# Expert output of 896 streamed and 1152 gathered columns, with second-half differences made by GpSimd

## The chip, the cores and the metric

The kernel runs on one core of a Trainium2 chip. The metric is the device time of one execution in microseconds (us), as a median over runs; lower is better. TensorE, VectorE, ScalarE and GpSimd are named PE, DVE, ACT and POOL in the profile, and SP is the queue that issues most of the plain DMAs.

## The reference

The reference is a three-layer model on 256 tokens of width 2048: a retention layer, a latent attention layer, and a layer with two kinds of attention followed by a mixture of 16384 small experts. The change touches only the end, the output of the experts. Cut to what matters:

```python
experts = i1 * 128 + i2                       # 128 picks a token: 8 heads x top 16
gates = softmax(top_vals)
u = take(expert_down, experts)                # (token, 128, 2048)
hdn = gelu(einsum('ted,td->te', u, x))
v = take(expert_up, experts)                  # (token, 128, 2048)
y = einsum('te,ted->td', gates * hdn, v)      # added to the residual
out = rms_norm(h + y, final_norm_gain)
```

All is float32. A token's output is the sum of 128 rows of `expert_up`, each scaled by one coefficient.

## The kernel before, in words

The 256 tokens are two halves of 128, `t` = 0 and 1, with one token on each partition. Each engine runs an instruction list of its own in program order; named semaphores (`built`, `rows_used`, ...) order the engines against each other. `sig.at(key)` is what a waiter waits for, `sig.to(key)` is what a producer raises.

**Down rows.** POOL gathers 256 times (`n` = 128 t + pick) one row of `expert_down` for each partition (line 625, `in_peer_down`), and DVE takes the product with the token's input (line 1611). This raises `rows_used` 0 to 255.

**Up rows, in two ways.** The 2048 output columns are split at `DCOL`. The right part, `D - DCOL` columns, is gathered: POOL fetches 256 times one row a partition into one of `NU` buffers (line 637, `in_up_rows`), and DVE adds it, scaled by the coefficient, to the residual `X` (line 1624), which raises `rows_used` 256 to 511. POOL may run `NU` gathers ahead of DVE. The left part, `DCOL` columns, is done as a dense product: all 16384 rows are streamed by SP as 128 blocks of 128 rows (line 573, `in_up_blocks`) through `NS` buffers, and PE multiplies each block by a coefficient matrix (line 2166). The sum over the 128 blocks stays in four PSUM banks.

**Coefficient matrices.** For that product every token's 128 coefficients have to stand at the place of their experts among 16384. An expert is (first half i1, second half i2). For four tokens at a time (a step `q`, 32 steps for each `t`) two 128 x 128 tables a token are made: `OH1`, in which pick e has its coefficient at column i1, and `OH2`, with a one at column i2. PE multiplies the two (line 2149, four products, raises `built`) and ACT copies the result out (line 981, `store`). The tables come from differences: `compare` lets PE write, for each half, pick number minus column number into a PSUM bank (lines 2125 and 2127, a pair for each half). For `t` = 0 ACT turns both differences into tables. For `t` = 1, the stage that the change is about, DVE makes `OH1` from its bank (line 1632, raises `first_hot_v`), and ACT makes `OH2` from its own (lines 999 and 1003, raise `second_hot`). Both have two buffers, so that step q waits for `built` of step q - 2.

**Order in the build stage of t = 1.** DVE's list interleaves the two jobs:

```python
if 2 <= n < 34:
    q = n - 2
    ...
    v.wait_ge(*built.at(fours[30 + q]))
```

`fours[30 + q]` is step q - 2 of `t` = 1. One scaled addition stands before each table. POOL's list holds only gathers in this stretch. When step 31 is built, PE spreads the final gain (line 2157) and then runs through the 128 blocks. At the end DVE adds the four banks to `X` (line 1640), ACT sums squares (lines 1015, 1022), and DVE scales and SP writes out.

Of the kernel before, what the change touches and what calls it, by code (L numbers as in the profile page):

```python
# [14 lines left out]
D = 2048  # L15
NG = 8
DCOL = 1024
NU = 6
NS = 4
EPS = 1e-6  # L20
# [92 lines left out]
def flat(x):  # L113
    return x.rearrange("p a b -> p (a b)")


def build(nc, A, out):
    ctx = ExitStack()
    with ctx:
# [137 lines left out]
        EF = [GBA[:, 512 + 256 * t:768 + 256 * t].rearrange("p (i j) -> p i j", i=2) for t in range(2)]  # L257
        EFR = [at(kept_end + 256 * t, 2, 128, of=arena_r) for t in range(2)]
        STEP, LESS, IDR, ONER = (at(kept_end + 512 + 128 * i, 128, of=arena_r if i else arena) for i in range(4))
        assert kept_end + 1024 <= LBO + 4 * 384, kept_end  # L260
        gbuf = [at(RAWS + i * 2048, D) for i in range(NG)]

        ubuf = [at(144 * KB + 1024 * i, D - DCOL) for i in range(2)] + [at(YG + 1024 * i, D - DCOL) for i in range(4)]
        sbuf = [at(W + 4096 + DCOL * i, DCOL) for i in range(NS)]
        OH1 = [at(152 * KB + 512 * i, 4, 128) for i in range(2)]
# [154 lines left out]
        d_g = [dma_sig(f"d_g{i}", range(32)) for i in range(NG)]  # L420
        d_u = [dma_sig(f"d_u{i}", range(43)) for i in range(NU)]
        d_s = [dma_sig(f"d_s{i}", range(32)) for i in range(NS)]

# [88 lines left out]
        first_hot_a, first_hot_v = sig("first_hot_a", fours[0:32]), sig("first_hot_v", fours[32:])  # L512
        compared, less_read, second_hot = sig("compared", fours), sig("less_read", fours), sig("second_hot", fours)
        built, stored = sig("built", fours), sig("stored", fours)
        block_used = sig("block_used", range(127))
# [30 lines left out]
        def sync(sp):  # L546
# [9 lines left out]
            for i, (kind, n, fn, info) in enumerate(plan):  # L556
# [10 lines left out]
                for dst, src in fn(raws[i % 8]):  # L567
                    sp.dma_start(dst, src).then_inc(wsem[i % 8], 16)
            sp.wait_ge(*gate_made.at(1))
            for b in range(128):  # L570
                if b >= NS:
                    sp.wait_ge(*block_used.at(b - NS))
                sp.dma_start(sbuf[b % NS], up_blocks[b]).then_inc(*d_s[b % NS].to(b // NS))
# [6 lines left out]
        def gpsimd(g):  # L580
# [38 lines left out]
            for n in range(256):  # L619
                i, t, j = n % NG, n // 128, n % 128  # L620
                if j % 64 == 0:
                    g.wait_ge(*chosen.at((t, j // 64)))
                if n >= NG:
                    g.wait_ge(*rows_used.at(n - NG))
                g.indirect_dma_start(  # L625
                    out=gbuf[i], out_offset=None, in_=down,
                    in_offset=bass.IndirectOffsetOnAxis(ap=EI[t][:, j:j + 1].bitcast(U32), axis=0)
                ).then_inc(*d_g[i].to(n // NG))
            for n in range(256):
                i, t, j = n % NU, n // 128, n % 128  # L630
                if n == 0:
                    g.wait_ge(*picks_rounded.at(1))
                elif n == 2:
                    g.wait_ge(*rows_used.at(255))
                if n >= NU:
                    g.wait_ge(*rows_used.at(256 + n - NU))
                g.indirect_dma_start(  # L637
                    out=ubuf[i], out_offset=None, in_=up_rows,
                    in_offset=bass.IndirectOffsetOnAxis(ap=EI[t][:, j:j + 1].bitcast(U32), axis=0)
                ).then_inc(*d_u[i].to(n // NU))  # L640


        def scalar(s):
# [329 lines left out]
            for t in range(2):  # L973
                s.wait_ge(*chosen.at((t, 1)))
                s.copy(flat(EFR[t]), flat(EF[t])).then_inc(*picks_rounded.to(t))  # L975

# [6 lines left out]

            for t in range(2):
                s.wait_ge(*rows_used.at(128 * t + 127))
                s.activation(HD[t], HD[t], ACT.Gelu_apprx_tanh).then_inc(*gelud.to(t))
# [4 lines left out]
                for q in range(33):  # L991
                    o1, o2 = OH1[q % 2], flat(OH2[q % 2])
                    if q < 32:
                        s.wait_ge(*compared.at((t, q)))
                        if 32 * t + q >= 2:
                            s.wait_ge(*built.at(fours[32 * t + q - 2]))
                        if t == 0:
                            s.activation(flat(o1), bank[q % 2], ACT.Abs)
                        s.activation(o2, bank[2 + q % 2], ACT.Abs).then_inc(*less_read.to((t, q)))
# [18 lines left out]
            for t in range(2):  # L1018
                for b in range(2):
                    c = 24 + 3 * t + 1 + b  # L1020
                    s.wait_ge(*dense_added.at(2 * t + b))
                    r = s.activation(GBB[:, 0:512], X[:, t, b * 512:(b + 1) * 512], ACT.Square, scale=float(D) ** -0.5,
                                     accum_out=st[:, c:c + 1])
# [7 lines left out]
        def vector(v):  # L1031
# [587 lines left out]
            for n in range(256):  # L1619
                t, j = n // 128, n % 128  # L1620
                v.wait_ge(*d_u[n % NU].at(n // NU))
                if n:
                    v.wait_ge(*rows_used.at(256 + n - 1))
                v.scalar_tensor_tensor(out=X[:, t, DCOL:], in0=ubuf[n % NU], scalar=HD[t][:, j:j + 1], in1=X[:, t, DCOL:],  # L1624
                                       op0=ALU.mult, op1=ALU.add).then_inc(*rows_used.to(256 + n))
                if 2 <= n < 34:
                    q = n - 2
                    if q == 0:
# [7 lines left out]
            for t in range(2):  # L1636
                for b in range(2):
                    xs = X[:, t, b * 512:(b + 1) * 512]
                    v.wait_ge(*dense_made.at(2 * t + b))
                    v.tensor_tensor(xs, bank[2 * t + b], xs, ALU.add).then_inc(*dense_added.to(2 * t + b))  # L1640
            v.wait_ge(*gain_made.at(0))
# [15 lines left out]
        def tensor(pe):  # L1657
# [460 lines left out]
            def compare(t, q):  # L2118

                if q == 0:  # L2120
                    pe.wait_ge(*picks_rounded.at(t))
                for p in range(2):
                    b = 2 * p + q % 2
# [5 lines left out]
                free[q % 2] = first_hot_v.at((1, q)) if t else less_read.at((0, q))  # L2129
                free[2 + q % 2] = less_read.at((t, q))  # L2130

            pe.wait_ge(*rounded.at(0))
            take(6)
            take(7)
            for t in range(2):
                compare(t, 0)
                take(4 + t)
# [24 lines left out]
            for i2 in range(128):  # L2162
                pe.wait_ge(*d_s[i2 % NS].at(i2 // NS))
                for t in range(2):
                    for b in range(2):
                        r = pe.matmul(bank[2 * t + b], coef_of(t, i2), sbuf[i2 % NS][:, b * 512:(b + 1) * 512],  # L2166
                                      start=i2 == 0, stop=i2 == 127)
# [38 lines left out]
```

## Time and profile before

| what | value |
|---|---|
| device time, median of 3 runs | 3396.77 us (3392.41 to 3396.88) |
| the profiled execution, its own time | 3395.3 us |
| its span, first to last instruction | 3393.5 us |
| gather of down rows ends (last of line 1611) | 2784.2 us |
| build stage of t = 1 | 2785 to 2932.6 us |
| stream of the up blocks on PE | 2938.6 to 3380.3 us |
| TensorE clock, mean over the span | 0.826 |

Times in the table are from the start of the span. The profile has rows for each instruction and, for a stretch, the busy time of every engine, the clock that TensorE was granted (1.00 is 2.4 GHz), the busy share of the 16 DMA engines and the bytes that they moved. An idle time in square brackets stands ahead of the instruction, with what ended it.

### The profile page before, as it was taken

Reading aid. Unit: us, or ns where it says so; the run is one execution under the profiler, and the core shown is the slowest. Engines: PE = TensorE matmul, PEld = TensorE weight load, DVE = VectorE, ACT = ScalarE, POOL = GpSimd, SP = SyncE. Lnnn points to the kernel's source line nnn. Section 1 sums busy time; section 2 is a strip of 40 time slices with the busy share of each in tenths; the row PEclk is TensorE's granted clock in tenths of the full one; section 3 lists DMA queues with packets and bytes.
Section 4 is the critical chain, followed back from the end, with each engine's and each line's share of the span. In section 5 each row is a group of like instructions: output and inputs, shape, how many; then the busy total and the mean of one; then the engine's idle time right before and its main releaser. Section 6 shows DMA issues by size and latency. Waiting matters only on the chain.

```text
span 3393.5 us, 34746 instructions
## 1 busy us (share of the span) xinstructions
PE 2632.1 (78%) x13316; PEld 2068.8 (61%) x13316; DVE 2259.6 (67%) x3026; ACT 1013.4 (30%) x1649; POOL 827.0 (24%) x581
## 2 busy tenths in 40 slices
PE   3789999989989989799997984000098019999998
PEld 3689999977869877798875884000055006544443
DVE  6877777776754455444434458999999984566666
ACT  2233433443444444443334441000087004200000
POOL 5500000000000000000000003733588871345443
PEclk9789999999999999798985987555555555699999
DMA  8768777767856435364330544999999994699998
GB/s 295 258 216 265 266 260 260 250 230 246 286 150 171 134 101 165 100 184 128 114 113 25 174 149 184 377 360 352 345 421 421 422 385 122 217 409 409 409 409 336
DMA packets 340693, 858.35 MB, mean 253 GB/s; under 512 B 38072, under 2 KB 97728, under 8 KB 306864
## 3 DMA queue, kind: packets, MB, share of 16 engines
q1 hardware_dynamic: 265872, 447.54, 39.8%
q0 software_dynamic: 74656, 408.60, 30.9%
q8 instruction: 105, 1.72, 0.2%
q14 instruction: 60, 0.49, 0.0%
HBM read 853.95 MB, written 2.10 MB: 252 GB/s over the span
## 4 chain that ended last, share of the span: by engine, by line
PE 52%; DVE 12%; POOL 8%; issue 3%; ACT 2%; DMA 1%; DVEq 0%; ACTq 0%; POOLq 0%
PE ps L2166 13%; PE ps L1666 10%; PE ps L1668 9%; PE ps L1667 9%; POOL s L625 8%; DVE s L1611 7%; PE ps L2149 2%; PE ps L2127 1%; PE ps L2046 1%; PE ps L2125 1%; PE ps L1927 1%; DMA s<-in_peer_down,s 1%; PE ps L2048 1%; DVE s L1521 0%; DVE s L1512 0%
## 5 line engine op out<-in xcount | busy, mean ns | idle before, releaser
L1666 PE MATMUL ps<-r,r 128*128 128x256 f32 (+2 forms) x3248 | 1065.5, 328 | 81.3 <-DVE r L1044 42.3
L1044 DVE TENSOR_TENSOR r<-s,r 128x1024 fp32r<-128x1024 f32 (+1 forms) x532 | 647.2, 1221 | 616.1 <-ACT r L652 615.6
L1667 PE MATMUL ps<-r,r 128*128 128x256 f32 (+2 forms) x3248 | 1047.2, 322 | 0.0
L1668 PE MATMUL ps<-r,r 128*128 128x256 f32 (+2 forms) x3248 | 1046.3, 322 | 0.0
L652 ACT CAST r<-s 128x1024 fp32r<-128x1024 f32 (+1 forms) x532 | 551.3, 1039 | 954.4 <-PE ps L1668 910.2
L1666 PEld LDWEIGHTS ps<-r,r 128*128 128x128 f32 x3248 | 642.7, 198 | 137.5 <-DVE r L1044 40.3
L1667 PEld LDWEIGHTS ps<-r,r 128*128 128x128 f32 x3248 | 643.1, 198 | 43.6 <-issue 4.6
L1668 PEld LDWEIGHTS ps<-r,r 128*128 128x128 f32 x3248 | 642.0, 198 | 41.0
L1611 DVE CUSTOM_DVE_ANT_0 s<-s,s 128x2048 f32<-128x2048 f32 x256 | 583.8, 2285 | 30.9 <-DMA s<-in_peer_down,s 30.7
L625 POOL DMA_INDIRECT s<-in_peer_down,s x256 | 473.1, 1848 | 448.6 <-DVE s L1569 238.0
L1624 DVE SCALAR_TENSOR_TENSOR s<-s,s,s 128x1024 f32<-128x1024 f32 x256 | 328.6, 1284 | 163.9 <-DMA s<-in_up_rows,s 162.4
L2166 PE MATMUL ps<-s,s 128*128 128x512 f32 x896 | 392.1, 595 | 0.0
L2125 PE MATMUL ps<-r 128*128 128x512 f32 x128 | 100.5, 785 | 353.7 <-ACT r L975 353.7
L637 POOL DMA_INDIRECT s<-in_up_rows,s x256 | 251.9, 984 | 346.6 <-DVE s L1624 323.1
L2166 PEld LDWEIGHTS ps<-s,s 128*128 128x128 f32 x896 | 170.9, 191 | 215.3 <-issue 215.3
L2125 PEld LDWEIGHTS ps<-r 128*128 128x128 f32 x128 | 39.8, 311 | 381.9 <-ACT r L972 353.9
L610 POOL DMA_DIRECT2D s<-in_final_norm_g x1 | 0.6, 625 | 1093.5 <-DVE s L1393 1093.5
L1062 DVE SCALAR_TENSOR_TENSOR s<-s,s,s 128x512 f32<-128x512 f32 x304 | 226.7, 783 | 2.5 <-DMA s<-in_ada_w 1.1
L2139 PE MATMUL ps<-s 128*128 128x128 f32 x2 | 0.9, 448 | 200.0 <-DVE s L1616 200.0
L2149 PE MATMUL ps<-s 128*128 128x128 f32 x512 | 132.4, 441 | 5.8 <-ACT s L1008 3.1
L2149 PEld LDWEIGHTS ps<-s 128*128 128x128 f32 x512 | 113.9, 327 | 33.3 <-issue 20.6
L1015 ACT ACTIVATE s<-s 128x1024 f32<-128x1024 f32 x2 | 2.1, 1056 | 442.3 <-DVE s L1624 442.3
(259 smaller groups left out, 2123.3 us busy)
## 6 DMA issues: line engine op xcount, KB each, us to landing
s<-in_ada_w SPq DMA_DIRECT2D x192, 512.0 KB, 5.4
s<-in_ret_w_in SPq DMA_DIRECT2D x128, 512.0 KB, 5.4
s<-in_up_blocks SPq DMA_DIRECT2D x128, 512.0 KB
s<-in_w_in SPq DMA_DIRECT2D x96, 512.0 KB, 3.7
s<-in_ret_w_in SPq DMA_DIRECT2D x128, 256.0 KB, 3.9
s<-in_ret_w_out SPq DMA_DIRECT2D x64, 512.0 KB, 5.1
s<-in_mla_w_in SPq DMA_DIRECT2D x48, 512.0 KB, 3.7
s<-in_mla_w_out SPq DMA_DIRECT2D x32, 512.0 KB, 3.7
```

What stands on the lines that cost most here:

```text
L625: g.indirect_dma_start(out=gbuf[i], out_offset=None, in_=down, in_offset=bass.IndirectOffsetOnAxis(ap=EI[t][:, j:j + 1].bitcast(U32), axis ...
L637: g.indirect_dma_start(out=ubuf[i], out_offset=None, in_=up_rows, in_offset=bass.IndirectOffsetOnAxis(ap=EI[t][:, j:j + 1].bitcast(U32), a ...
L652: s.copy(hi_of(w), raw_of(w)).then_inc(*hi_made.to(w))
L1044: v.tensor_tensor(lo_of(w), raw_of(w), hi_of(w).bitcast(F), ALU.subtract).then_inc(*lo_made.to(w))
L1062: r = v.scalar_tensor_tensor(out=acc[h], in0=w, scalar=cact[:, k:k + 1], in1=acc[h], op0=ALU.mult, op1=ALU.add)
L1611: v.tensor_tensor_reduce(gbuf[n % NG], gbuf[n % NG], HN[:, t, :], 1.0, 0.0, ALU.mult, ALU.add, HD[t][:, j:j + 1]).then_inc(*rows_used.to(n))
L1624: v.scalar_tensor_tensor(out=X[:, t, DCOL:], in0=ubuf[n % NU], scalar=HD[t][:, j:j + 1], in1=X[:, t, DCOL:], op0=ALU.mult, op1=ALU.add).th ...
L1666: pe.matmul(o, lh, rh, start=start, stop=False, skip_group_check=True)
L1667: pe.matmul(o, lh, rl, start=False, stop=False, skip_group_check=True)
L1668: return pe.matmul(o, ll, rh, start=False, stop=stop, skip_group_check=True)
L2149: r = pe.matmul(bank[b][:, k * 128:(k + 1) * 128], OH1[q % 2][:, k, :], OH2[q % 2][:, k, :], start=True, stop=True)
L2166: r = pe.matmul(bank[2 * t + b], coef_of(t, i2), sbuf[i2 % NS][:, b * 512:(b + 1) * 512], start=i2 == 0, stop=i2 == 127)
```

## The change

`DCOL` goes from 1024 to 896. So a block of the stream has 896 columns (448 for each of the four products of a block), and a gathered row has 1152. The gathered rows have 5 buffers in place of 6, the stream 3 in place of 4, and both lie elsewhere. In the build stage of `t` = 1 DVE does two scaled additions for each table. The second difference there is no longer written by PE: PE turns the second halves of the picks once, ACT copies them to `SECOND`, and POOL subtracts them from the column numbers (`less`), straight into `OH2`, where ACT works in place. `less` stands in POOL's list behind every second gather. The diff, cut to its core:

```diff
-DCOL = 1024
-NU = 6
-NS = 4
+DCOL = 896
+HCOL = DCOL // 2
+NU = 5
+NS = 3
...
         def sync(sp):
             sp.wait_ge(*gate_made.at(1))
+            sp.wait_ge(*picks_rounded.at(1))
+            sp.wait_ge(*second_copied.at(0))
             for b in range(128):
...
         def gpsimd(g):
+            def less(q):
+
+                g.wait_ge(*built.at(fours[30 + q]))
+                g.tensor_tensor(OH2[q % 2], STEP.unsqueeze(1).broadcast_to([128, 4, 128]),
+                                SECOND[:, 4 * q:4 * q + 4].unsqueeze(2).broadcast_to([128, 4, 128]),
+                                ALU.subtract).then_inc(*second_less.to((1, q)))
+
+            g.wait_ge(*gate_made.at(1))
             for n in range(256):
                 i, t, j = n % NU, n // 128, n % 128
-                if n == 0:
-                    g.wait_ge(*picks_rounded.at(1))
-                elif n == 2:
+                if n == 2:
+                    g.wait_ge(*second_copied.at(0))
+                    g.wait_ge(*d_step.at("all"))
+                    less(0)
+                    less(1)
                     g.wait_ge(*rows_used.at(255))
                 if n >= NU:
                     g.wait_ge(*rows_used.at(256 + n - NU))
...
                 ).then_inc(*d_u[i].to(n // NU))
+                if n % 2 == 0 and 2 <= n // 2 < 32:
+                    less(n // 2)
...
         def scalar(s):
                     if q < 32:
-                        s.wait_ge(*compared.at((t, q)))
-                        if 32 * t + q >= 2:
-                            s.wait_ge(*built.at(fours[32 * t + q - 2]))
-                        if t == 0:
+                        if t:
+                            s.wait_ge(*second_less.at((1, q)))
+                            s.activation(o2, o2, ACT.Abs).then_inc(*less_read.to((t, q)))
+                        else:
...
         def vector(v):
                 v.scalar_tensor_tensor(out=X[:, t, DCOL:], in0=ubuf[n % NU], scalar=HD[t][:, j:j + 1], in1=X[:, t, DCOL:],
                                        op0=ALU.mult, op1=ALU.add).then_inc(*rows_used.to(256 + n))
-                if 2 <= n < 34:
-                    q = n - 2
+                if n % 2 and n // 2 - 1 in range(32):
+                    q = n // 2 - 1
                     if q == 0:
                         v.wait_ge(*coef_copied.at(1))
                     v.wait_ge(*built.at(fours[30 + q]))
...
         def tensor(pe):
-                for p in range(2):
+                for p in range(2 - t):
                     b = 2 * p + q % 2
...
+                if t:
+                    take(5)
+                    pe.transpose(bank[5][:, 0:128], EF[1][:, 1, :], IDN).then_inc(*second_turned.to(0))
+                    free[5] = second_copied.at(0)
                 compare(t, 0)
```

The rows below are instruction lists, without times; names in brackets are the semaphores that a row waits for. POOL, at the end of the down gathers and the start of the up gathers, before (`in_up_rows` is the gathered part, `s144_57` and `s112_55` hold its buffers):

```order
L637 DMA s144_57<-in_up_rows,s192_60 128x1024 [waits picks_rounded]
L637 DMA s144_57<-in_up_rows,s192_60 128x1024
L637 DMA s112_55<-in_up_rows,s192_60 128x1024 [waits rows_used]
L637 DMA s112_55<-in_up_rows,s192_60 128x1024 x3
L637 DMA s144_57<-in_up_rows,s192_60 128x1024 [waits rows_used] x2
L637 DMA s112_55<-in_up_rows,s192_60 128x1024 [waits rows_used] x4
```

The same place on POOL in the changed kernel, where line 653 is the gather and line 638 is `less`:

```order
L653 DMA s160_58<-in_up_rows,s192_60 128x1152 [waits gate_made]
L653 DMA s160_58<-in_up_rows,s192_60 128x1152
L638 TENSOR_TENSOR s144_57<-s192_60 128x512 [waits built,d_step,second_copied]
L638 TENSOR_TENSOR s144_57<-s192_60 128x512 [waits built]
L653 DMA s112_55<-in_up_rows,s192_60 128x1152 [waits rows_used]
L653 DMA s112_55<-in_up_rows,s192_60 128x1152 x2
L638 TENSOR_TENSOR s144_57<-s192_60 128x512 [waits built]
L653 DMA s160_58<-in_up_rows,s192_60 128x1152 [waits rows_used] x2
L638 TENSOR_TENSOR s144_57<-s192_60 128x512 [waits built]
L653 DMA s112_55<-in_up_rows,s192_60 128x1152 [waits rows_used] x2
```

Gathers 0 and 1 stand ahead of `less` 0 and 1, then come gathers 2, 3 and 4, `less` 2, gathers 5 and 6, `less` 3, and so on up to `less` 31 behind gather 62: every second gather now stands behind an instruction that waits for `built`.

DVE, at the start of the build stage of `t` = 1, before (line 1624 is the scaled addition, line 1632 the table `OH1`; `d_u0` and the like are the gathers' landings):

```order
L1624 SCALAR_TENSOR_TENSOR s0_49<-s144_57,s192_60,s0_49 128x1024 [waits d_u0,coef_made]
L1624 SCALAR_TENSOR_TENSOR s0_49<-s144_57,s192_60,s0_49 128x1024 [waits rows_used,d_u1]
L1624 SCALAR_TENSOR_TENSOR s0_49<-s112_55,s192_60,s0_49 128x1024 [waits rows_used,d_u2]
L1632 SCALAR_TENSOR_TENSOR s144_57<-ps,s192_60 128x512 [waits compared,built,coef_copied]
L1624 SCALAR_TENSOR_TENSOR s0_49<-s112_55,s192_60,s0_49 128x1024 [waits rows_used,d_u3]
L1632 SCALAR_TENSOR_TENSOR s144_57<-ps,s192_60 128x512 [waits compared,built]
L1624 SCALAR_TENSOR_TENSOR s0_49<-s112_55,s192_60,s0_49 128x1024 [waits rows_used,d_u4]
L1632 SCALAR_TENSOR_TENSOR s144_57<-ps,s192_60 128x512 [waits compared,built]
```

The same place on DVE in the changed kernel (line 1648 the addition, line 1656 the table):

```order
L1648 SCALAR_TENSOR_TENSOR s0_49<-s160_58,s192_60,s0_49 128x1152 [waits d_u0,coef_made]
L1648 SCALAR_TENSOR_TENSOR s0_49<-s160_58,s192_60,s0_49 128x1152 [waits rows_used,d_u1]
L1648 SCALAR_TENSOR_TENSOR s0_49<-s112_55,s192_60,s0_49 128x1152 [waits rows_used,d_u2]
L1648 SCALAR_TENSOR_TENSOR s0_49<-s112_55,s192_60,s0_49 128x1152 [waits rows_used,d_u3]
L1656 SCALAR_TENSOR_TENSOR s144_57<-ps,s192_60 128x512 [waits compared,built,coef_copied]
L1648 SCALAR_TENSOR_TENSOR s0_49<-s112_55,s192_60,s0_49 128x1152 [waits rows_used,d_u4]
L1648 SCALAR_TENSOR_TENSOR s0_49<-s160_58,s192_60,s0_49 128x1152 [waits rows_used,d_u0]
L1656 SCALAR_TENSOR_TENSOR s144_57<-ps,s192_60 128x512 [waits compared,built]
L1648 SCALAR_TENSOR_TENSOR s0_49<-s160_58,s192_60,s0_49 128x1152 [waits rows_used,d_u1]
```

Table 0 stood behind addition 2 and now stands behind addition 3, table 1 behind addition 5 in place of 3; in general table q stands behind addition 2q + 3 in place of q + 2.

## Rows read from the trace of the kernel before

**Rows 1.** The chain that ended last, from 2922 us on: start us, us, what

```profile
2924.29 2.01 PE ps L2149 x8
2926.30 0.43 PE ps L2125
2926.72 0.72 PE ps L2127
2927.44 0.73 PE ps L2125
2928.17 0.72 PE ps L2127
2928.89 3.69 PE ps L2149 x16
...
2933.51 5.06 PE ps L2157 x32
2938.57 441.72 PE ps L2166 x1024
...
3380.31 0.70 DVE s L1640
```

**Rows 2.** Busy time, clock, DMA share and GB/s, by stretches

```profile
2784.00:2938.50 154.50, 149.75 (x414) 94.98 (x414) 71.62 (x76) 60.43 (x130) 43.01 (x43) 0.51 0.44 138
2938.50:3380.00 441.50, 441.50 (x1025) 195.26 (x1024) 278.87 (x219) 3.65 (x8) 204.52 (x212) 1.00 1.01 401
...
2938.50:2942.00 3.50, 3.50 (x5) 1.50 (x5) 3.29 (x3) 0.00 (x0) 2.59 (x4) 0.50 0.95 341
...
3000.00:3300.00 300.00, 300.00 (x701) 132.82 (x700) 188.48 (x148) 1.15 (x2) 142.56 (x147) 1.00 1.03 409
3300.00:3380.00 80.00, 80.00 (x188) 35.20 (x186) 50.05 (x41) 2.50 (x6) 30.01 (x33) 1.00 0.94 374
```

The columns are the stretch and its length, then PE, PE's weight loads, DVE, ACT and POOL, each with its instructions, then clock, DMA share and GB/s.

**Rows 3.** Groups of instructions in the build stage, 2784 to 2938.5 us

```profile
L637 POOL DMA_INDIRECT s<-in_up_rows,s x43 | 43.2, 1004 | 122.8 <-DVE s L1624 107.2 <-DVE s L1611 11.9 <-issue 3.7
L1632 DVE SCALAR_TENSOR_TENSOR s<-ps,s 128x512 f32<-128x512 f32 x32 | 22.1, 691 | 79.7 <-PE ps L2127 79.7
```

**Rows 4.** Groups of instructions in the stream, 2938.5 to 3380 us

```profile
L1624 DVE SCALAR_TENSOR_TENSOR s<-s,s,s 128x1024 f32<-128x1024 f32 x216 | 277.5, 1285 | 161.2 <-DMA s<-in_up_rows,s 160.4
```

**Rows 5.** Timeline at the start of the build stage, PE, DVE and POOL

```profile
2784.59 0.93 POOL L637 DMA_INDIRECT s<-in_up_rows,s  x1 [11.88 <-DVE s L1611]
2785.03 2.68 DVE L1624 SCALAR_TENSOR_TENSOR s<-s,s,s 128x1024 f32<-128x1024 f32 x2
...
2785.83 1.29 POOL L637 DMA_INDIRECT s<-in_up_rows,s  x1 [0.30 <-issue]
...
2788.86 1.28 DVE L1624 SCALAR_TENSOR_TENSOR s<-s,s,s 128x1024 f32<-128x1024 f32 x1 [1.15 <-DMA s<-in_up_rows,s]
2790.06 0.69 DVE L1632 SCALAR_TENSOR_TENSOR s<-ps,s 128x512 f32<-128x512 f32 x1
...
2790.85 2.04 PE L2149 MATMUL ps<-s 128*128 128x128 f32 x8 [2.67 <-issue]
...
2791.64 1.28 DVE L1624 SCALAR_TENSOR_TENSOR s<-s,s,s 128x1024 f32<-128x1024 f32 x1 [0.89 <-DMA s<-in_up_rows,s]
...
2792.93 0.65 ACT L981 COPY s<-ps 128x256 f32<-128x256 f32 x2 [3.45 <-issue]
```

**Rows 6.** POOL's two-input operation in the first layer, ns min/median/max

```profile
L606 POOL TENSOR_TENSOR s<-s x24: 1260/1340/2905, 23.6 to 175.8; 128x512 f32<-128x512 f32 x24
```

**Rows 7.** Timeline at the first gather of down rows

```profile
2083.99 1.03 POOL L625 DMA_INDIRECT s<-in_peer_down,s  x1 [237.98 <-DVE s L1569]
...
2089.83 2.29 DVE L1611 CUSTOM_DVE_ANT_0 s<-s,s 128x2048 f32<-128x2048 f32 x1 [6.73 <-DMA s<-in_peer_down,s]
```

**Rows 8.** Timeline behind the last table: additions whose gathers had landed

```profile
2929.61 12.39 DVE L1624 SCALAR_TENSOR_TENSOR s<-s,s,s 128x1024 f32<-128x1024 f32 x9
```

**Rows 9.** Timeline within the stream: a gather's issue, and its addition six later

```profile
3000.49 0.94 POOL L637 DMA_INDIRECT s<-in_up_rows,s  x1 [1.60 <-DVE s L1624]
...
3011.61 1.28 DVE L1624 SCALAR_TENSOR_TENSOR s<-s,s,s 128x1024 f32<-128x1024 f32 x1 [0.80 <-DMA s<-in_up_rows,s]
```

More of the change, by code:

```diff
@@ L257, in build @@
         EF = [GBA[:, 512 + 256 * t:768 + 256 * t].rearrange("p (i j) -> p i j", i=2) for t in range(2)]
-        EFR = [at(kept_end + 256 * t, 2, 128, of=arena_r) for t in range(2)]
+        EFR = [at(kept_end + 256 * t, 2 - t, 128, of=arena_r) for t in range(2)]
+        SECOND = at(kept_end + 384, 128)
         STEP, LESS, IDR, ONER = (at(kept_end + 512 + 128 * i, 128, of=arena_r if i else arena) for i in range(4))
@@ L261, in build @@
         gbuf = [at(RAWS + i * 2048, D) for i in range(NG)]
-        ubuf = [at(144 * KB + 1024 * i, D - DCOL) for i in range(2)] + [at(YG + 1024 * i, D - DCOL) for i in range(4)]
-        sbuf = [at(W + 4096 + DCOL * i, DCOL) for i in range(NS)]
+        ubuf = [at(W + 4096 + (D - DCOL) * i, D - DCOL) for i in range(2)] + [at(YG + (D - DCOL) * i, D - DCOL) for i in range(3)]
+        sbuf = [at(144 * KB + DCOL * i, DCOL) for i in range(2)] + [at(W + 4096 + 2 * (D - DCOL), DCOL)]
         OH1 = [at(152 * KB + 512 * i, 4, 128) for i in range(2)]
@@ L420, in build @@
         d_g = [dma_sig(f"d_g{i}", range(32)) for i in range(NG)]
-        d_u = [dma_sig(f"d_u{i}", range(43)) for i in range(NU)]
-        d_s = [dma_sig(f"d_s{i}", range(32)) for i in range(NS)]
+        d_u = [dma_sig(f"d_u{i}", range(52)) for i in range(NU)]
+        d_s = [dma_sig(f"d_s{i}", range(43)) for i in range(NS)]
         hi_made = sig("hi_made", range(NW))
@@ L513, in build @@
         compared, less_read, second_hot = sig("compared", fours), sig("less_read", fours), sig("second_hot", fours)
+        second_turned, second_copied = sig("second_turned", [0]), sig("second_copied", [0])
+        second_less = sig("second_less", fours[32:])
         built, stored = sig("built", fours), sig("stored", fours)
@@ L974, in scalar @@
                 s.wait_ge(*chosen.at((t, 1)))
-                s.copy(flat(EFR[t]), flat(EF[t])).then_inc(*picks_rounded.to(t))
+                s.copy(flat(EFR[t]), flat(EF[t][:, 0:2 - t, :])).then_inc(*picks_rounded.to(t))
             def store(t, q):
@@ L984, in scalar @@
             for t in range(2):
+                if t:
+                    s.wait_ge(*second_turned.at(0))
+                    s.copy(SECOND, bank[5][:, 0:128]).then_inc(*second_copied.to(0))
                 s.wait_ge(*rows_used.at(128 * t + 127))
@@ L993, in scalar @@
                     if q < 32:
-                        s.wait_ge(*compared.at((t, q)))
-                        if 32 * t + q >= 2:
-                            s.wait_ge(*built.at(fours[32 * t + q - 2]))
-                        if t == 0:
+                        if t:
+                            s.wait_ge(*second_less.at((1, q)))
+                            s.activation(o2, o2, ACT.Abs).then_inc(*less_read.to((t, q)))
+                        else:
+                            s.wait_ge(*compared.at((t, q)))
+                            if q >= 2:
+                                s.wait_ge(*built.at((0, q - 2)))
                             s.activation(flat(o1), bank[q % 2], ACT.Abs)
-                        s.activation(o2, bank[2 + q % 2], ACT.Abs).then_inc(*less_read.to((t, q)))
+                            s.activation(o2, bank[2 + q % 2], ACT.Abs).then_inc(*less_read.to((t, q)))
                         s.wait_ge(*less_read.at((t, q)))
@@ L1021, in scalar @@
                     s.wait_ge(*dense_added.at(2 * t + b))
-                    r = s.activation(GBB[:, 0:512], X[:, t, b * 512:(b + 1) * 512], ACT.Square, scale=float(D) ** -0.5,
+                    r = s.activation(GBB[:, 0:HCOL], X[:, t, b * HCOL:(b + 1) * HCOL], ACT.Square, scale=float(D) ** -0.5,
                                      accum_out=st[:, c:c + 1])
@@ L1637, in vector @@
                 for b in range(2):
-                    xs = X[:, t, b * 512:(b + 1) * 512]
+                    xs = X[:, t, b * HCOL:(b + 1) * HCOL]
                     v.wait_ge(*dense_made.at(2 * t + b))
-                    v.tensor_tensor(xs, bank[2 * t + b], xs, ALU.add).then_inc(*dense_added.to(2 * t + b))
+                    v.tensor_tensor(xs, bank[2 * t + b][:, 0:HCOL], xs, ALU.add).then_inc(*dense_added.to(2 * t + b))
             v.wait_ge(*gain_made.at(0))
@@ L2129, in compare @@
                 free[q % 2] = first_hot_v.at((1, q)) if t else less_read.at((0, q))
-                free[2 + q % 2] = less_read.at((t, q))
+                if t == 0:
+                    free[2 + q % 2] = less_read.at((0, q))
             pe.wait_ge(*rounded.at(0))
@@ L2135, in tensor @@
             for t in range(2):
+                if t:
+                    take(5)
+                    pe.transpose(bank[5][:, 0:128], EF[1][:, 1, :], IDN).then_inc(*second_turned.to(0))
+                    free[5] = second_copied.at(0)
                 compare(t, 0)
@@ L2165, in tensor @@
                     for b in range(2):
-                        r = pe.matmul(bank[2 * t + b], coef_of(t, i2), sbuf[i2 % NS][:, b * 512:(b + 1) * 512],
+                        r = pe.matmul(bank[2 * t + b][:, 0:HCOL], coef_of(t, i2), sbuf[i2 % NS][:, b * HCOL:(b + 1) * HCOL],
                                       start=i2 == 0, stop=i2 == 127)
```

## The prediction

> **What bounds the kernel now.** I read the chain that ended last first, since it names what the end of the program hangs on. From 2924 us to 3380 us it is TensorE alone [rows 1]. The reader sees two stages there. In the build stage of t = 1 one step takes 4.60 us (2924.29 to 2928.89): 2.01 us for the four products, and 2.60 us for two pairs of difference products. Then the stream takes 441.7 us for 1024 matmul instructions, 0.4314 us each. The view by stretches says what stands beside it [rows 2]. In the build stage the DMA engines are busy 0.44 of the time. In the stream TensorE is busy in all of its 441.5 us at clock 1.00, and the DMA engines are full as well: 409 GB/s between 3000 and 3300 us. So the stream is held by TensorE with the transfers just behind it, and VectorE waits there 160 us for gathered rows [rows 4]. The build stage is held by TensorE with idle transfers: VectorE waits for a difference product 79.7 us, and GpSimd 107 us for an addition [rows 3].
>
> **Part 1, the stream.** A matmul instruction covers 448 columns for 512, so TensorE needs 1024 x 0.4314 x 0.875 = 386.5 us. The transfers: a block is 128 x 896 x 4 = 0.459 MB, a gather 128 x 1152 x 4 = 0.590 MB (0.524 MB each before). Both numbers matter, since TensorE alone would give back 55 us and the transfers won't.
>
> **Part 2, the build step on each engine.** TensorE loses one pair, 1.45 us of 4.60 [rows 1], and comes to 3.15. VectorE: an addition of 1024 columns takes 1.285 us [rows 4] and 12.39 / 9 = 1.377 us in a row with its overhead [rows 8]; 128 columns more at 1.28 / 1024 us each make it 1.51. Two and a table of 0.69 [rows 3] are 3.7 us. GpSimd: `less` is two-input work on 128 x 512 floats; the trace has the same shape in an addition at 1.34 us, 1.26 to 2.91 [rows 6]. With two gathers at 0.94 and 0.30 between instructions [rows 5, 9] that is 3.8 to 4.1 us. By busy time, then, a step would come to about 4.1 us and the stage would be no longer than now.
>
> **Part 3, the order, which decides.** Table q stands behind addition 2q + 3, and that needs gather 2q + 3. On GpSimd this gather stands behind `less(q + 1)`, which waits for `built` of step q - 1. And `built` of step q waits for table q. So from one `built` to the next everything is in series: `less`, gather issue, landing, addition, table, products. No buffer count loosens it, because GpSimd's list holds the gather back and not a full buffer. Behind the waiting `less(q + 1)` are queued gathers 2q + 3 and 2q + 4, and VectorE waits for them. Before, no gather stood behind `built`. Price of a turn:
> - `built` to the start of `less`: 0.10, an estimate between 0.04 (ACT's copy at 2792.93 behind products that end at 2792.89) and 0.27 us (a gather at 2784.59 behind VectorE) [rows 5].
> - `less`: 1.34, alone on the engines at that moment, since VectorE has finished addition 2q + 2 during the products. Bounds 1.26 and 2.91 [rows 6].
> - gap to the issue: 0.30 [rows 5].
> - issue to the start of its addition: gather 2 was issued at 2784.59 with nothing in flight, and its addition began at 2788.86 after waiting for it: 4.27 us [rows 5]. The wider row adds 0.066 MB at 409 GB/s, 0.16: 4.43. From below: issue of 0.93 and 0.59 MB at 409 GB/s, 2.4 us. From above: the first gather of down rows, 1.05 MB, 5.84 us [rows 7]. I stay with 4.43, the same kind of gather with one just behind it.
> - addition to table: 2788.86 to 2790.06 is 1.20; with 128 more columns 1.33. Table to products 0.79, products 2.04 [rows 5].
>
> The sum is 10.33 us a turn against 4.60.
>
> A landing by the Trainium skill ("DMA: Bandwidth & Descriptors", Anatomy of one DMA, its fit for one gather) would be 2.0 us plus bytes at 436 GB/s, 3.35 us for 0.59 MB, against 4.27 us for the smaller gather in this trace. By it a turn would be 9.25 us and the final time about 32 us under mine; the trace has the duration, so I use that.
>
> **The sum.** Additions 0 and 1 and gathers 2 to 4 start as before. Addition 3 began at 2791.64 [rows 5], now some 0.2 later; table 0 follows at 2793.1, its products end at 2796.0. Thirty turns (gather 63 is the last behind a `less`) are 310 us: `built` of step 30 at 2796 + 310 = 3106. Step 31 needs additions 64 and 65, no `less` between: 3.5 us, 3109.5. The 6.0 us from the last products' end (2928.89 + 3.69) to the stream at 2938.57 stay [rows 1]: stream start 3115.5, 177 us later than before.
>
> Its length: by then some 72 additions are done (66, and six at 1.51 from 3106.6 on) and two more gathers have landed. Left are 182 gathers, 107.3 MB, and 125 blocks, 57.3 MB: 164.7 MB at 409 GB/s are 402.7 us. The whole stream moved 177.0 MB at a mean of 401, where 409 would have needed 432.8; 8.7 us went in its slower start and end (341 and 374 GB/s) [rows 2], and I add them: 411 us. TensorE's 386.5 us lie inside, and the gathers end last. Check by queue: in 386.5 us the blocks take 148 GB/s and leave 261, a gather each 2.26 us, 171 of them; 11 more at VectorE's 1.51 us are 17 us, 403 and the ends. So the stream gives back 441.5 - 411 = 30 us, not 55.
>
> The end: now the last addition follows the last landing (1.4 us), and three bank additions precede the last one (2 us for 448 columns each). Last bank addition 3115.5 + 411 + 3.4 = 3530, and 13.2 us as from 3380.3 to 3393.5: span 3543. Device time stands 1.8 us over the span (3395.3 to 3393.5), so 3545 us; the profiled execution lies 1.5 us under the median, which I leave. The rest costs nothing: the one transpose and ACT's copy of it sit in 168 us in which TensorE is idle (hidden by down gathers; in the open they are below 1 us), `less` 0 and 1 run while GpSimd waits 11.9 us for the last down row [rows 5], and the first blocks load later but 170 us before use.
>
> **Rivals.**
> - *The ring doesn't close* (the change does what busy time allows): I have misread which gather stands behind which `less`, and the step is 4.1 us. For it speaks only Part 2; against it, both lists. 32 steps end at 2790 + 131 + 3, stream from 2930, 30 us shorter, 3.4 later at the end: about 3359 us, faster. The point from which it decides: the stream and the end together give back 30 - 3 = 27 us, so even with the ring the change is no loss if a turn takes no more than (2938.5 + 27 - 2796 - 9.5) / 30 = 5.3 us. Without any gather the ring has 0.10 + 1.34 + 1.33 + 0.79 + 2.04 = 5.6. Chance 4%.
> - *A shorter landing*: issue to addition between 2.4 and 3.7 us. A turn shortens by as much, thirty times: 3.7 gives 3523 us, 2.4 gives 3484. For it speaks that gather 2 had three more behind it in row, where a turn has one; against it, that gather 3, issued 1.24 us later, was not ready before 2791.6 [rows 5]. 13%.
> - *`less` at its slow price*, 2.91 us as when VectorE works beside it: + 1.57 x 30 = 47, 3592 us. Against it, VectorE idles then. 8%.
> - *Three stream buffers are too few*. A gather under full load took 3000.49 to 3011.61, 11.1 us [rows 9]. Were a block as slow (9.5 us with one gather fewer in flight), a block would take (3.0 + 9.5) / 3 = 4.2 us while gathers last: blocks take 0.459 MB / 4.2 us = 109 GB/s, and 182 gathers at 0.590 MB by the other 300 GB/s, 1.97 us, are 359 us and 86 blocks; the other 42 at 3.0 are 127: 486 us, + 75, 3620. Against it: before, four buffers gave a block 10.4 us to land and TensorE never waited; a block needs less than half the bytes of the traffic. 12%.
> - *The clock*: the stream's first 3.5 us ran at 0.50 and then at 1.00 [rows 2], 1.2 against 2.4 GHz. If gaps kept it at 0.50 throughout, TensorE would need 773 us and the end would be near 3905. Before it rose after a build stage at 0.51. 2%.
>
> The forecast has 60%, with 3525 to 3565 of its own, and 1% is left for no change. I take 3495 to 3605 as the range: it holds the forecast, most of the shorter landings and the slow `less`, and leaves out the ring that doesn't close, the full starvation and the clock. A difference of 0.2%, about 7 us, is what a measurement tells here: faster 4%, same 1%, slower 95%.
>
> **What would show it.** In the profile after: the build stage some 320 us long with a step near 10.3 us; TensorE busy for a third of it; VectorE's idle time there put down to gathers, and GpSimd's to the products of line 2178 (`built`), 30 times; DMA share below 0.4. In the stream: about 410 us, DMA at 409 GB/s, TensorE done some 20 us before the last addition. The prediction is wrong if the step is near 4 to 5 us (the ring), or if the turn is right and the stream is not 400 to 425 us (the sharing of the DMA engines).

## The result, and the profile after

The changed kernel takes 3555.11 us (median of 4 runs, 3543.64 to 3556.44); the kernel before, run beside it, takes 3394.59 us (3391.61 to 3396.88). The ratio is 1.0466, with a 95% interval of 1.0442 to 1.049: 160 us slower, where 148 had been forecast (3545 against 3396.77). The profiled execution of the changed kernel is the shortest of the four; its first down row is taken at 2078.4 us where before it was 2089.8 [rows 7], in a part of the program that is the same in both. The lengths of the stages don't depend on that, and I compare these.

The view by stretches of the changed kernel, with columns as in [rows 2]:

```profile
2776.00:3095.00 319.00, 107.75 (x351) 79.02 (x350) 118.66 (x103) 60.66 (x128) 105.62 (x102) 0.50 0.40 132
3095.00:3100.00 5.00, 5.00 (x8) 2.51 (x8) 4.30 (x4) 0.00 (x0) 3.56 (x3) 0.50 0.90 293
...
3150.00:3400.00 250.00, 234.29 (x591) 107.14 (x589) 164.18 (x116) 1.26 (x2) 164.24 (x116) 1.00 1.02 407
...
3495.00:3529.00 34.00, 33.70 (x90) 16.72 (x88) 2.46 (x5) 2.89 (x7) 0.00 (x0) 1.00 0.39 122
```

The first row is the build stage: 319 us in place of 154.5, TensorE busy for a third of it, the transfers for 0.40 of it. No engine is busy half of the time, the sign of a chain through several of them. The third row is the stream with full DMA engines, in which TensorE is busy for 94% and no longer for all. The last row is new: the gathers are over, and for 34 us TensorE works through leftover blocks alone.

The waits of the build stage (engine and line, what it waited for: us in total, times, longest):

```profile
DVE s L1648 <- DMA s<-in_up_rows,s: 199.0, 62, 6.6
POOL s L638 <- PE ps L2178: 196.4, 30, 7.1
```

Before, VectorE waited for TensorE and GpSimd for VectorE [rows 3]. Now `less` (line 638) waits thirty times for `built` (line 2178), 6.5 us each, and VectorE's additions wait for gathers. One turn in the timeline of the changed kernel:

```profile
2942.30 2.05 PE L2178 MATMUL ps<-s 128*128 128x128 f32 x8 [7.07 <-issue]
...
2944.43 1.04 POOL L638 TENSOR_TENSOR s<-s 128x512 f32<-128x512 f32 x1 [6.88 <-PE ps L2178]
...
2945.61 0.94 POOL L653 DMA_INDIRECT s<-in_up_rows,s  x1
...
2946.86 0.94 POOL L653 DMA_INDIRECT s<-in_up_rows,s  x1 [0.30 <-issue]
2950.01 1.42 DVE L1648 SCALAR_TENSOR_TENSOR s<-s,s,s 128x1152 f32<-128x1152 f32 x1 [6.49 <-DMA s<-in_up_rows,s]
2951.35 0.68 DVE L1656 SCALAR_TENSOR_TENSOR s<-ps,s 128x512 f32<-128x512 f32 x1
...
2952.13 2.05 PE L2178 MATMUL ps<-s 128*128 128x128 f32 x8 [6.64 <-issue]
...
2954.26 1.04 POOL L638 TENSOR_TENSOR s<-s 128x512 f32<-128x512 f32 x1 [6.45 <-PE ps L2178]
```

Products end at 2944.35, `less`, gather, its addition, the table, and products again until 2954.18: 9.83 us, everything in series. In the whole stage the first table stands at 2783.0 and the last at 3084.1, 9.71 us a step.

In the stream TensorE waits for blocks. From the view of the line that loads them (line 579), who waited for it (us, times) and how long a block took from issue to landing. PEld is the loading of weights, which runs beside the matmuls, so the first two rows overlap and don't add up:

```profile
PEld ps L2195: 93.0, 112
PE ps L2195: 26.5, 48
DMA to landing us min/median/max: 3.0/6.7/14.9
```

### The profile page after: what moved, and what is told of

Same layout as the page of the kernel before. It is cut to its first block, busy times and chain, and to the rows that moved or that the text cites. A ratio compares the mean times of both kernels' runs of the same rounds, so it can differ in the third digit from the quotient of the medians.

```text
span 3541.8 us, 34623 instructions
## 1 busy us (share of the span) xinstructions
PE 2545.4 (72%) x13253; PEld 2038.5 (58%) x13253; DVE 2293.2 (65%) x3026; ACT 1014.4 (29%) x1650; POOL 939.9 (27%) x613
## 4 chain that ended last, share of the span: by engine, by line
PE 41%; DVE 12%; DMA 8%; issue 8%; POOL 7%; ACT 2%; DVEq 0%; ACTq 0%; POOLq 0%
PE ps L1690 9%; PE ps L1691 9%; PE ps L1692 9%; DVE s L1635 7%; POOL s L631 7%; DMA s<-in_up_blocks 7%; PE ps L2195 5%; PE ps L2178 2%; DMA s<-in_peer_down,s 1%; PE ps L2070 1%; PE ps L1951 1%; PE ps L2151 1%; PE ps L2072 0%; DVE s L1545 0%; DVE s L1536 0%
## 5 line engine op out<-in xcount | busy, mean ns | idle before, releaser
L1648 DVE SCALAR_TENSOR_TENSOR s<-s,s,s 128x1152 f32<-128x1152 f32 x256 | 363.3, 1419 | 338.0 <-DMA s<-in_up_rows,s 336.1
L2195 PE MATMUL ps<-s,s 128*128 128x448 f32 x984 | 392.4, 550 | 26.1 <-DMA s<-in_up_blocks 25.6
L653 POOL DMA_INDIRECT s<-in_up_rows,s x256 | 337.5, 1318 | 162.9 <-DVE s L1648 98.6
L2149 PE MATMUL ps<-r 128*128 128x512 f32 x96 | 75.0, 781 | 353.9 <-ACT r L993 353.9
L2195 PEld LDWEIGHTS ps<-s,s 128*128 128x128 f32 x984 | 181.0, 191 | 235.3 <-issue 146.6
L2149 PEld LDWEIGHTS ps<-r 128*128 128x128 f32 x96 | 30.6, 318 | 368.1 <-ACT r L990 354.0
```

Source lines behind the costliest of these rows:

```text
L653: g.indirect_dma_start(out=ubuf[i], out_offset=None, in_=up_rows, in_offset=bass.IndirectOffsetOnAxis(ap=EI[t][:, j:j + 1].bitcast(U32), a ...
L2195: r = pe.matmul(bank[2 * t + b][:, 0:HCOL], coef_of(t, i2), sbuf[i2 % NS][:, b * HCOL:(b + 1) * HCOL], start=i2 == 0, stop=i2 == 127)
```

## The experiments

Times are medians, with the ratio to the kernel before that ran beside each, and its 95% interval; a step is the time from the first table to the last, over 31, in the profiled execution.

| kernel | time, us | ratio | step, us | stream start to end of span, us |
|---|---|---|---|---|
| before | 3394.6 | | 4.48 | 455.0 |
| changed | 3555.1 | 1.0466 (1.0442 to 1.049) | 9.71 | 446.8 |
| `less` one later | 3453.9 | 1.0168 (1.0151 to 1.0184) | 6.53 | 447.8 |
| `less` three later | 3405.6 | 1.003 (1.0018 to 1.0043) | 4.81 | 449.1 |
| table one addition earlier | 3452.2 | 1.0175 (1.016 to 1.019) | 6.50 | 448.2 |
| four stream buffers | 3538.2 | 1.0416 (1.0398 to 1.0433) | 9.71 | 429.4 |
| columns alone | 3413.8 | 1.005 (1.0035 to 1.0065) | 4.48 | 479.3 |
| three later and four buffers | 3386.1 | 0.9983 (0.9973 to 0.9993) | 4.84 | 430.0 |
| one addition, 1024 | 3351.4 | 0.9876 (0.9862 to 0.9891) | 3.08 | 456.1 |
| one addition, 896 | 3390.8 | 0.9984 (0.9974 to 0.9993) | 3.08 | 488.8 |
| two additions, 1024 | 3398.2 | 1.0012 (1.0001 to 1.0022) | 4.49 | 455.0 |
| three for two, 960 | 3371.0 | 0.9927 (0.9913 to 0.9941) | 3.83 | 448.5 |

**Is it the order? `less` one gather later.**

```diff
-                if n % 2 == 0 and 2 <= n // 2 < 32:
-                    less(n // 2)
+                if n % 2 == 1 and 2 <= (n - 1) // 2 < 32:
+                    less((n - 1) // 2)
```

> One gather is moved: `less(q)` stands behind gather 2q + 1 in place of 2q, so gather 2q + 3 no longer stands behind `less(q + 1)` but behind `less(q)`. Theory A (the order on GpSimd closes a ring of one turn): the ring now spans two steps, 9.9 us and one more gather issue of 1.24 us over two steps, 5.6 us a step. The build stage shortens by 30 x 4.3 = 129 us from 321 to about 192, the time comes to 3426 us (3415 to 3445). Theory B (the amount of work of a step, two wider additions from five buffers, sets it, wherever `less` stands): nothing moves, step 9.9 us, 3545 to 3560 us.

Measured: 3453.9 us, 101 us under the changed kernel, with the same instructions in every list. A step went from 9.71 to 6.53 us. Theory B, that the amount of work sets the step, is out. Theory A has the mechanism, but the time lies 28 us above its figure and outside its range. Two steps of this kernel in the timeline show why (VectorE, TensorE and GpSimd, rows in between left out):

```profile
2881.18 1.04 POOL L638 TENSOR_TENSOR s<-s 128x512 f32<-128x512 f32 x1 [0.76 <-PE ps L2178]
...
2883.62 1.19 POOL L653 DMA_INDIRECT s<-in_up_rows,s  x1 [0.30 <-issue]
...
2887.10 2.05 PE L2178 MATMUL ps<-s 128*128 128x128 f32 x8 [4.86 <-issue]
...
2889.34 2.15 DVE L1648 SCALAR_TENSOR_TENSOR s<-s,s,s 128x1152 f32<-128x1152 f32 x1 [0.16 <-DMA s<-in_up_rows,s]
...
2890.42 1.89 POOL L653 DMA_INDIRECT s<-in_up_rows,s  x1
...
2892.19 2.04 PE L2178 MATMUL ps<-s 128*128 128x128 f32 x8 [1.89 <-issue]
...
2900.22 2.05 PE L2178 MATMUL ps<-s 128*128 128x128 f32 x8 [4.84 <-issue]
```

Steps of 5.1 us (products at 2887.10 and 2892.19) and 8.0 us (2892.19 to 2900.22) take turns. Two steps are 13.1 us where I had 11.2: gather 2q + 3, issued at 2883.62, has another just ahead of it and its addition starts only at 2889.34, 5.7 us later and not 4.4; and that addition runs beside `less` and takes 2.15 us in place of 1.42.

**`less` three gathers later** is the same edit with 3 for 1 (and `n % 2 == 1`).

> `less(q)` behind gather 2q + 3. Theory A: the ring spans three steps, (9.9 + 1.2) / 3 = 3.7 us, so it no longer binds; GpSimd's own work does, 1.04 for `less` and two gathers of 0.94 to 1.5 us with 0.3 between, 3.8 to 4.8 us a step. Build stage 150 to 180 us in place of 321, time 3375 to 3410 us, VectorE's waits for gathers in the stage below 60 us in place of 199. Theory B: 3545 to 3560 us, as before it.

Measured: 3405.6 us, a step of 4.81 us, just above what GpSimd's own work had been priced at. `less` waits for `built` once in the stage, 4.1 us, in place of thirty times and 196 us; VectorE's waits for gathers in the stage are 35 us in place of 199, and over all 256 additions 169 in place of 336. Of the 160 us that the change cost, this edit alone gives 149 back.

**From the other side: the table one addition earlier**, and GpSimd's list as changed.

```diff
-                if n % 2 and n // 2 - 1 in range(32):
+                if n % 2 == 0 and n // 2 - 1 in range(32):
```

> The ring is opened from the other side: GpSimd's list stays as changed, and on VectorE table q stands behind addition 2q + 2 in place of 2q + 3. That addition's gather stands ahead of `less(q + 1)`. Theory A (the order): the same ring over two steps as with `less` one gather later, which measured 6.53 us a step; step 6.2 to 6.9 us, build stage 210 to 235 us, time 3454 us (3440 to 3470). Rival D (the gain there came from GpSimd having more gathers in flight, not from the ring): the number of gathers that GpSimd has issued when `less` waits is unchanged here, so the step stays at 9.9 us and the time at 3540 to 3557 us.

Measured: 3452.2 us and 6.50 us a step, within 2 us of the twin on GpSimd's side, and at the forecast. Only the relation between the two lists counts, so the ring is shown and not just argued.

**A fourth stream buffer.**

```diff
-NS = 3
+NS = 4
...
-        sbuf = [at(144 * KB + DCOL * i, DCOL) for i in range(2)] + [at(W + 4096 + 2 * (D - DCOL), DCOL)]
+        sbuf = [at(144 * KB + DCOL * i, DCOL) for i in range(2)] + [at(W + 4096 + 2 * (D - DCOL) + DCOL * i, DCOL) for i in range(2)]
```

> A fourth buffer for the streamed blocks, nothing else (three leave a block two blocks' time, 6.05 us, to land, and the profile after shows a median of 6.7). Theory S (three buffers starve TensorE and so leave blocks over when the gathers are done): waits of TensorE for blocks fall from 47 us to below 10, stream 434 us to about 411, time 20 to 25 us under the changed kernel, about 3532 us; build stage 321 us unmoved. Theory T (the DMA engines are full until the last gather in any case and the gathers take their share first): TensorE's waits stay, less than 6 us come back, 3549 to 3557 us.

Measured: 3538.2 us, 17 us under the changed kernel, a little less than the 20 to 25 expected. Its stretches:

```profile
3106.90:3495.00 388.10, 388.02 (x1025) 195.67 (x1024) 241.77 (x171) 1.26 (x2) 168.48 (x172) 0.99 1.02 405
3495.00:3521.00 26.00, 0.00 (x0) 0.00 (x0) 20.58 (x17) 0.46 (x1) 16.21 (x11) 0.57 0.82 285
```

TensorE no longer waits (388.0 of 388.1 us busy) and is done first; the last 26 us belong to the gathers. From the stream's start at 3106.9 the last addition starts 412.1 us later, at 3519.0, and ends after 413.5 us. Theory S holds: a block lands 6.7 us after its issue in the changed kernel, and three buffers allow 2 x 3.03 = 6.05 us. The Trainium skill ("DMA: Bandwidth & Descriptors", Queues, rings and completion order) says that a DMA engine takes turns between the queues that have work, packet by packet. No run here shows whether they do: between 3150 and 3480 us of the changed kernel, with up to five gathers pending, a block took 6.7 us to land and a gather 8.6, of which 1.5 is its instruction on GpSimd, and two figures so near each other fit turns as well as one common line.

**The columns alone**: the kernel before with `DCOL = 896`, `HCOL`, `NU = 5`, `NS = 3` and the buffers where the change has them, and otherwise the lists of before.

> The kernel before with 896 streamed and 1152 gathered columns and 3 and 5 buffers, but with one addition for each table and both differences by TensorE as before. Theory A: build stage as before, 154 us; some 211 gathers of 0.59 MB are left at its end, 124 MB and 57 MB of blocks, 182 MB at 409 GB/s = 444 us, some more with three stream buffers, where TensorE alone would take 387. Time 3395 to 3425 us: the columns give nothing without additions moved into the build stage. Theory C (TensorE alone holds the stream): 442 - 387 = 55 us come back, 3340 to 3355 us.

Measured: 3413.8 us, 19 us slower than before. The build step is that of before (4.48 us). The stream with its end takes 24 us more: 55 us less work for TensorE, and nothing of it arrives, since the transfers hold the stream: 397 GB/s over its length, and the last addition starts at 3390.4 where TensorE's last matmul starts at 3369.3. Theory C is out. This run has three stream buffers; the run below with one addition, 896 columns and four says the same without that doubt.

**`less` three later and the fourth buffer together.** Both edits from above.

> `less` three gathers later and a fourth stream buffer together. Theory A with theory S (two separate losses, one in each stage, that add up): build stage 170 us as with `less` three later alone, stream and end 429 us as with four buffers alone, time 3388 us (3382 to 3394), 17 us under the former. Rival (the losses overlap: gathers brought forward take the place of what the fourth buffer gives): 3398 to 3406 us.

Measured: 3386.1 us, within the range; 19.5 us under the edit to the order alone, where the buffer had given 17 in the changed kernel. The two losses lie in two stages and add up. With both mended the change is faster than before by 0.17%, hardly more than a measurement can tell.

**One addition for each table, 1024 columns.** Of the change only GpSimd's differences are left.

```diff
-DCOL = 896
-NU = 5
-NS = 3
+DCOL = 1024
+NU = 6
+NS = 4
...
-                if n % 2 == 0 and 2 <= n // 2 < 32:
-                    less(n // 2)
+                if 2 <= n - 4 < 32:
+                    less(n - 4)
...
-                if n % 2 and n // 2 - 1 in range(32):
-                    q = n // 2 - 1
+                if 2 <= n < 34:
+                    q = n - 2
```

(With the buffers back in their places; the gathered rows then start behind `picks_rounded` and `second_copied`.)

> Of the change only GpSimd's differences are kept: 1024 columns, 6 and 4 buffers and one addition for each table as before, `less(q)` behind gather q + 4 so that no table's gather stands behind a `less` that needs the table before. Theory A (the difference pair taken from TensorE is worth 1.45 us a step where the order lets it): step 3.15 to 3.5 us, build stage 154 - 31 x 1.3 = 114 us, stream 442 us as before, 3355 us (3348 to 3370). Rival (GpSimd's work beside VectorE and its gathers is what a step waits for whatever the order): step 4.4 us and more, 3388 us or more.

Measured: 3351.4 us, 1.24% faster than before and the best of all. A step is TensorE's work again, as its timeline shows:

```profile
2833.56 2.08 PE L2177 MATMUL ps<-s 128*128 128x128 f32 x8
...
2835.28 0.77 PE L2148 MATMUL ps<-r 128*128 128x512 f32 x1
...
2835.72 1.04 POOL L636 TENSOR_TENSOR s<-s 128x512 f32<-128x512 f32 x1 [1.02 <-PE ps L2177]
2835.99 0.79 PE L2150 MATMUL ps<-r 1*128 1x512 f32 x1
2836.71 2.08 PE L2177 MATMUL ps<-s 128*128 128x128 f32 x8
```

3.15 us from products to products, 1.45 less than before, just the pair of difference products that left. `less` waits 1.02 us for TensorE, and nobody waits long for it.

**One addition, 896 columns**: the same additions and differences with the changed kernel's columns and the fourth stream buffer.

> As the former, with 896 and 1152 columns, 5 gather and 4 stream buffers. Theory A: build stage 114 us as there, but some 209 gathers are left at its end, 123 MB and 57 MB of blocks, 442 us at 409 GB/s and 9 more at the ends: the stream is held by transfers at 451 us, time 3368 us (3360 to 3380), 13 us above the former. Rival C (TensorE holds the stream): 387 us, 3310 us.

Measured: 3390.8 us, 23 us above theory A's figure, though with its order: the build step is as forecast, and the stream is held by gathers and not by TensorE, which is done at 3287 us of 3388.9. The size was off in the last part. When the blocks are through, the gathers alone go like this (columns as in [rows 2]):

```profile
3290.00:3370.00 80.00, 0.00 (x0) 0.00 (x0) 61.74 (x44) 0.00 (x0) 59.24 (x43) 0.50 0.92 326
```

44 additions in 80 us, 1.82 us each at 326 GB/s, where I had taken VectorE's 1.51 us or 409 GB/s. Some forty gathers at 0.3 us more are 12 of the 23 us. Most of the other 11 is a wrong count: from the stream's start to the start of the last addition 184 MB moved, with 215 gathers where I had 209 and some 180 MB, and that is about 8 us at 409 GB/s.

**Two additions, 1024 columns**, `less` three later, 6 and 4 buffers.

> Two additions for each table and `less(q)` behind gather 2q + 3, with 1024 columns, 6 and 4 buffers. Theory A: the step is held by GpSimd and VectorE at 4.6 to 4.8 us, build stage 165 us; the stream is held by TensorE at 442 us, so that the additions brought forward give nothing: 3406 us (3398 to 3413), slower than before. Rival (gathers brought forward shorten the stream at any columns): 3375 us or less.

Measured: 3398.2 us, the lower edge of the range. The step came out at 4.49 us and not 4.6 to 4.8, and the stream at before's 455.0 us: VectorE is done at 3308 us, 66 us ahead of TensorE, and gets nothing for it. So two additions buy nothing at 1024 columns, and they cost 1.4 us a step against one. At 896 columns, with four stream buffers in both, two additions take 3386.1 us and one 3390.8: there they pay, by 5 us.

**Three additions for two tables, 960 columns.** `less(q)` behind gather 4 + 3q/2, table q behind addition 2 + 3q/2.

> From the version with one addition a table (3351 us): three additions for two tables, 960 and 1088 columns, 5 gather and 4 stream buffers, `less(q)` behind gather 4 + 3q/2. VectorE has 1.5 x 1.45 + 0.69 = 2.9 us of work a step, GpSimd 1.04 + 1.5 x 1.24 + 0.3 = 3.2, TensorE 3.15: step 3.2 to 3.5 us, build stage 112 to 122 us. Stream: some 200 gathers of 0.557 MB and 125 blocks of 0.492 MB are 173 MB, 422 us and 9 at the ends, where TensorE needs 414. Theory A: 3344 us (3336 to 3356), at best level with or 10 us under the version with one addition. Rival (GpSimd has no slack left and the landing is back in the step): step 4 us and more, 3365 us or more.

Measured: 3371.0 us, 20 us above the version with one addition: nearer to the rival's. The stream is as priced (448.5 us with its end). The step is 3.83 us and not 3.2 to 3.5, and from the end of the last down row to the stream it is 135 us where the build stage had been put at 112 to 122. `less` never waits there, so GpSimd has no slack left, as the rival said. The rival's second half, that the landing is back in the step, isn't so: between 2800 and 2910 us the chain that ended last runs through GpSimd's instructions for 93% and through no landing. What I had mis-sized is the gather's issue: priced at 0.94 us, it takes 1.82 at the median between 2790 and 2908 us.

## Why the prediction was right

**What bounds the kernel.** Right: before, TensorE held both stages, the stream with the transfers right behind. The columns alone show the second half of it.

**The order, which decides.** Right, as a mechanism and nearly in size. The ring was read out of two instruction lists, and it is there in the waits (30 times), in the timeline, and in the runs that open it: 9.71, 6.53, 4.81 us a step as `less` moves back by none, one and three gathers, 6.50 as the table moves forward by one. The rival in which the ring doesn't close (4%, 4.1 us a step and 3359 us) is out for the kernel as changed. With the ring opened by three gathers the kernel still takes 4.81 us a step and 3405.6 us, so that rival's price was too low as well.

**Price of a turn.** 10.33 us forecast, 9.83 in the timeline above and 9.91 as the mean of thirty (tables at 2783.0 and 3080.3). The landing was right, 4.40 for 4.43 (2945.61 to 2950.01). The landing by the fit of the Trainium skill ("DMA: Bandwidth & Descriptors", Anatomy of one DMA), an estimate of 3.35 us, would have missed the trace's 4.40 by a us. `less` was mis-sized: 1.04 us for 1.34, taken from an addition of the same shape in the first layer, and the gap behind it 0.14 for 0.30. VectorE's work explains only a part of the former: in the kernel before, the addition of the first layer that starts at 53.11 us takes 1.26 us though VectorE is idle beside it. What makes the rest isn't shown. Addition to table 1.34 for 1.33, table to products 0.78 for 0.79, products 2.05 for 2.04. Thirty turns made the miss 12.6 us.

**Stream start.** Forecast 177 us later. From the end of the last down row (2784.3 before, 2774.4 after) to the stream it is 154.2 and 320.6 us: 166 later. Some 2.4 us of what the turns gained was lost behind the ring: from the last `built` of the thirty turns to the stream it is 11.9 us for my 9.5, most of it in the spread of the gain, 7.16 us where before it took 5.06 [rows 1].

**The length of the stream.** Here a step failed: "TensorE's 386.5 us lie inside, and the gathers end last". In the changed kernel the gathers end first, 3495 us, and TensorE at 3529, 434 us after the start for my 411. The rival with too few stream buffers, given 12% and 75 us, came true in a milder form. My check by queue had let the blocks have all they ask for. The run with four buffers restores that premise, and its last addition starts after 412.1 us, so 411 was a fair price for a stream without starved blocks. In the changed kernel the lack costs 17 us in time.

**The sum.** +177 - 27 = +150 was forecast on the span, +166 - 8 = +158 measured by the stages, and 160 between the medians. So the total was only 8 us off by the stages because two misses of 11 and 19 us had opposite signs; each is larger than the error of the sum.

**The other rivals.** A shorter landing: no. `less` at 2.91 us: no, it was 1.04 to 1.06 in every turn, since VectorE was idle; where the order is opened it does meet VectorE (below). The clock: no, 0.50 in the stream's first 5 us, 0.95 in the next 5 and then 1.00, and TensorE's gaps, 6% of the time between 3150 and 3400 us, left it there.

## What to carry to other kernels

When work moves to another engine, write the two lists side by side and follow one buffer and one token round: an instruction that waits for the end of a step holds back everything queued behind it, and a DMA issue there puts the whole landing (4.4 us here) into every step, however idle the engines look. The cure was to put the waiting instruction a few issues later, at no cost in work. And before taking work off an engine that is full, look at what is full beside it: 55 us of TensorE's stream bought nothing while 409 GB/s stood behind it, and 1.45 us a step in a stage with idle transfers bought 42 us.

## What the runs showed that I had not expected

**VectorE and GpSimd stretch each other.** In the changed kernel, where they take turns, an addition of 128 x 1152 takes 1.406 to 1.481 us and `less` 1.039 to 1.055. With `less` three gathers later they overlap (line, operation and count: ns min/median/max):

```profile
L638 POOL TENSOR_TENSOR s<-s x32: 1042/1060/2087, 2771.6 to 2937.3; 128x512 f32<-128x512 f32 x32
...
L1648 DVE SCALAR_TENSOR_TENSOR s<-s,s,s x256: 1401/1418/2816, 2785.4 to 3352.1; 128x1152 f32<-128x1152 f32 x128
```

and in its timeline:

```profile
2878.94 2.09 POOL L638 TENSOR_TENSOR s<-s 128x512 f32<-128x512 f32 x1
...
2883.22 2.71 DVE L1648 SCALAR_TENSOR_TENSOR s<-s,s,s 128x1152 f32<-128x1152 f32 x1 [0.41 <-DMA s<-in_up_rows,s]
...
2883.65 1.05 POOL L638 TENSOR_TENSOR s<-s 128x512 f32<-128x512 f32 x1
2884.86 1.89 POOL L653 DMA_INDIRECT s<-in_up_rows,s  x1 [0.16 <-issue]
```

Of a pair that meets, one takes up to twice its time: `less` 2.09 us beside an addition and a table, or an addition 2.71 us beside `less` and the gather issue behind it. The Trainium skill ("GPSIMD Engine Reference", 1. Specifications) has GpSimd's SBUF interfaces shared with VectorE and names VectorE instructions with two SBUF inputs as a case of contention; the addition is one. The trace agrees so far as the long ones are those that overlap: 1.42 and 1.04 us alone, 2.71 and 2.09 beside the other engine. The gather's issue on GpSimd gets longer too: its median in the build stage is 0.945 us in the changed kernel, 1.60 with `less` three gathers later and 1.82 with three additions for two tables. The ring had hidden this, and that steps of 4.81 and 3.83 us stay above what each engine's own work adds up to is probably its doing; no run here takes the contention away to show it.

**A lone stream of gathers moves less than gathers and blocks together**: with one addition and 896 columns, 326 GB/s at a DMA share of 0.92 from five buffers of 0.59 MB once the blocks are through, and 409 GB/s at 1.03 with blocks beside them. Which part of the difference is the number of transfers in flight and which the kind of transfer isn't shown.
